# The delta rule's gate columns with TensorE's operands exchanged

## The reference, cut to what matters

```
h = rms_norm(x, mix_pre_norm[l])
proj = h @ w_in                      # (256, 1024) @ (1024, D_IN)
(dn_qkv, dn_z, dn_b, dn_a, ...) = jnp.split(proj, ...)   # dn_b, dn_a: 4 columns each
qkv = silu(causal_depthwise_conv(dn_qkv, dn_conv))
beta = sigmoid(dn_b)
g = -exp(dn_A_log) * softplus(dn_a + dn_dt_bias)
o_dn = gated_delta_rule(q, k, v, beta, g)
```

## Time and profile before

| what | us |
|---|---|
| three runs, median | 1917.99 |
| three runs, lowest and highest | 1915.57, 1919.57 |
| the profiled execution | 1917.77 |
| its span in the profile | 1916.0 |

### The profile page before, as it was taken

How to read it: one execution, slowest core, us unless ns; L and a number is a source line. 1 busy time by engine, 2 the same in 40 slices (tenths; PEclk the granted TensorE clock), 3 DMA queues, 4 the chain that set the end, 5 groups by cost and what they waited for, 6 DMA issues and landing times.

```text
span 1916.0 us, 35058 instructions
## 1 busy us (share of the span) xinstructions
PE 1888.3 (99%) x14788; PEld 1806.2 (94%) x14788; DVE 1252.2 (65%) x1678; ACT 956.3 (50%) x1381; POOL 308.2 (16%) x176
## 2 busy tenths in 40 slices
PE   7999999999999999999999999999999999999998
PEld 7999998998899999999989999999999899999998
DVE  6884567665689545777648775576647694567643
ACT  5634456444563345564445445555534445556533
POOL 0050221000003103200001352320001352221000
PEclk9999999999999999999999999999999999999999
DMA  6443344666545323555565553456655663445553
GB/s 227 160 143 111 112 154 153 205 195 209 163 135 165 111 99 122 201 173 190 193 195 176 183 187 122 133 181 190 191 187 171 218 193 115 136 169 187 186 188 100
DMA packets 92156, 317.50 MB, mean 166 GB/s; under 512 B 11744, under 2 KB 12896, under 8 KB 91744
## 3 DMA queue, kind: packets, MB, share of 16 engines
q1 hardware_dynamic: 91424, 314.69, 50.2%
q10 hardware_dynamic: 576, 0.57, 0.1%
HBM read 304.99 MB, written 1.05 MB: 160 GB/s over the span
## 4 chain that ended last, share of the span: by engine, by line
PE 84%; DVE 11%; ACT 2%; DMA 1%; issue 1%; SPq 0%; DVEq 0%; ACTq 0%
PE bank L2001 82%; DVE wlo L1126 4%; DVE area L1126 3%; DVE area L1132 1%; DMA raw<-in_weights 1%; ACT area L630 1%; PE bank L2512 1%; DVE hl L1132 1%; DVE xT L1132 1%; ACT whi L636 1%; PE bank L2220 1%; DVE area L1645 1%; DVE area L1643 0%; PE bank L2530 0%; ACT L618 0%
## 5 line engine op out<-in xcount | busy, mean ns | idle before, releaser
L1126 DVE TENSOR_TENSOR wlo<-raw,whi 128x1024 fp32r<-128x1024 f32 x518 | 666.3, 1301 | 402.6 <-ACT whi L636 402.2
L2001 PE MATMUL bank<-hh,whi 128*128 128x256 f32 x2928 | 834.5, 286 | 15.1 <-DVE wlo L1126 11.7
L2001 PE MATMUL bank<-hh,wlo 128*128 128x256 f32 x2928 | 818.2, 280 | 0.0
L2001 PE MATMUL bank<-hl,whi 128*128 128x256 f32 x2928 | 811.3, 280 | 0.0
L636 ACT CAST whi<-raw 128x1024 fp32r<-128x1024 f32 x572 | 589.4, 1046 | 415.7 <-PE bank L2001 369.9
L2001 PEld LDWEIGHTS bank<-hh,whi 128*128 128x128 f32 x2928 | 555.7, 190 | 28.4 <-DVE wlo L1126 15.1
L2001 PEld LDWEIGHTS bank<-hl,whi 128*128 128x128 f32 x2928 | 555.2, 191 | 1.9 <-issue 1.9
L2001 PEld LDWEIGHTS bank<-hh,wlo 128*128 128x128 f32 x2928 | 556.0, 190 | 0.0
L1781 POOL TENSOR_TENSOR area<-area 128x512 f32<-128x512 f32 (+4 forms) x86 | 136.7, 1596 | 567.8 <-DVE area L1132 249.8
L1781 POOL TENSOR_TENSOR wlo<-raw,whi 128x1024 fp32r<-128x1024 f32 x54 | 134.3, 2488 | 427.9 <-ACT whi L636 427.9
L2001 PE MATMUL bank<-area 128*128 128x128 f32 (+5 forms) x1544 | 199.9, 288 | 1.2 <-DVE area L1196 0.7
(11 more groups left out here) (127 smaller groups left out, 1918.3 us busy)
## 6 DMA issues: line engine op xcount, KB each, us to landing
raw<-in_weights SPq DMA_DIRECT2D x572, 512.0 KB, 4.1
area<-area SPq DMA_DIRECT2D x96, 64.0 KB, 3.6
area<-area SPq DMA_DIRECT2D x16, 128.0 KB, 4.0
cst<-in_const SPq DMA_DIRECT2D x1, 1188.0 KB, 8.3
cst<-in_const SPq DMA_DIRECT2D x1, 1024.5 KB, 6.9
xT<-in_x SPq DMA_DIRECT2D x4, 256.0 KB, 8.1
out<-xT SPq DMA_DIRECT2D x4, 256.0 KB, 2.9
area<-in_lev SPq DMA_DIRECT2D x2, 384.0 KB, 6.6
```

Source lines behind the costliest of these rows:

```text
L1126: return v.tensor_tensor(dst, x, y, op)
L2001: return e.matmul(ps, x, y, start=start, stop=stop, skip_group_check=skip)
```

## The change

The gate weights become the stationary operand, 16 columns (high and low side by side) for `hh` and 8 for `hl`, and 256 tokens are the other operand: 16 matmuls, whose sum is a 16 x 256 array in bank 1, rows 0 to 7 high by all, rows 8 to 15 low by high. They run after step 2 (behind the norm's sum) instead of after step 3. VectorE copies the 16 x 256 array to `ABR` (in plain fp32) in its hook, for which it waits. After step 3 TensorE multiplies each half of `ABR` as weights (16 x 128) with a 16 x 8 matrix, two identity matrices over each other, which transposes and adds the two halves in one; it is appended to `small` in 8 columns, so that tile grows from 576 to 584 columns. VectorE's product with the factor reads bank 1 at once. The cast and the subtraction of `SW` move out of the hooks, to between steps 1 and 2.

```diff
-N_SMALL = 64 + 512
+N_SMALL = 64 + 512 + 8
...
+        ABR = SM[0:16, 0:256]
...
                 def hook():
                     factor(norm)
-                    a.wait_ge(s_small[L], 16)
-                    a.copy(SW[:, :, 0:8], sm3).then_inc(*a_dn.up("SW", L))
...
                 next(qkv)
                 next(qkv)
+                a.wait_ge(s_small[L], 16)
+                a.copy(SW[:, :, 0:8], sm3).then_inc(*a_dn.up("SW", L))
                 next(qkv)
                 next(qkv)
...
                 def hook():
                     factor(norm)
-                    v.wait_ge(*a_dn.at("SW", L))
-                    tt(SW[:, :, 8:16], sm3, SW[:, :, 0:8].bitcast(F32), OP.subtract).then_inc(*v_dn.up("SW", L))
+                    v.wait_ge(*e_dn.at("abrow", L))
+                    v.tensor_copy(ABR, bank[1][0:16, 0:256]).then_inc(*v_dn.up("abrow", L))
...
                 next(qkv)
                 next(qkv)
+                v.wait_ge(*a_dn.at("SW", L))
+                tt(SW[:, :, 8:16], sm3, SW[:, :, 0:8].bitcast(F32), OP.subtract).then_inc(*v_dn.up("SW", L))
                 next(qkv)
                 next(qkv)
-                two = bank[1][:, 0:32].rearrange("p (s c) -> p s c", s=2)
                 v.wait_ge(*e_dn.at("ab", L))
-                v.tensor_copy(tmp2, two[:, :, 8:16]).then_inc(*v_dn.up())
-                v.wait_ge(*v_dn.now())
-                tt(AB2, two[:, :, 0:8], tmp2, OP.add).then_inc(*v_dn.up("absum", L))
-                v.wait_ge(*v_dn.now())
                 v.wait_ge(*v_norm.at("turned", norm))
-                tt(AB2, AB2, wide(RST[:, :], 2, 8), OP.mult).then_inc(*v_dn.up("ab", L))
+                tt(AB2, bank[1][:, 256:272].rearrange("p (s c) -> p s c", s=2), wide(RST[:, :], 2, 8), OP.mult).then_inc(*v_dn.up("ab", L))
...
                 next(qkv)
                 next(qkv)
                 next(qkv)
+                e.wait_ge(*v_dn.at("SW", L))
+                fresh(1, v_dn.at("ab", L))
+                for k in range(8):
+                    mm(bank[1][0:16, 0:T], SW[:, k, :], hh[:, k, :], k == 0, False, True)
+                    x = mm(bank[1][0:8, 0:T], SW[:, k, 0:8], hl[:, k, :], False, k == 7, True)
+                x.then_inc(*e_dn.up("abrow", L))
                 next(qkv)
-                e.wait_ge(*v_dn.at("SW", L))
-                fresh(1, v_dn.at("absum", L))
+                e.wait_ge(*v_dn.at("abrow", L))
                 for s in range(2):
-                    for k in range(8):
-                        mm(bank[1][:, 16 * s:16 * s + 16], hh[:, k, 128 * s:128 * s + 128], SW[:, k, :], k == 0, False, True)
-                        x = mm(bank[1][:, 16 * s:16 * s + 8], hl[:, k, 128 * s:128 * s + 128], SW[:, k, 0:8], False, k == 7, True)
+                    x = mm(bank[1][:, T + 8 * s:T + 8 * s + 8], ABR[:, 128 * s:128 * s + 128], small[0:16, 576:584], True, True)
                 x.then_inc(*e_dn.up("ab", L))
...
+        small[l][0:16, 576:584] = np.tile(np.eye(8, dtype=np.float32), (2, 1))
```

More of the change, by code:

```diff
@@ L398, in program @@
         u1, u2 = SM[:, 128:136], SM[:, 144:152]
-        AB2, tmp2 = (SM[:, c:c + 16].rearrange("p (s c) -> p s c", s=2) for c in (192, 224))
+        AB2 = SM[:, 192:208].rearrange("p (s c) -> p s c", s=2)
         AB = SM[:, 192:208].rearrange("p (s c) -> p c s", s=2)
+        ABR = SM[0:16, 0:256]
         sm3 = small[:, 0:64].rearrange("p (k c) -> p k c", c=8)
```

## The result

The changed kernel takes 1937.96 us (median of 4 runs, 1934.9 to 1938.49), the kernel before beside it 1916.78 (4 runs, 1913.67 to 1919.57): ratio 1.0117, 95% interval 1.0098 to 1.0137. The profiled execution took 1937.57, its span is 1935.8. I had said 1914.8, in a range from 1909.5 to 1918.8.

What follows compares the result with a forecast made beforehand. TensorE, busy 99%, was taken as the bound, with VectorE limiting its gain at the end of `qkv`. 1917.77 minus 1.1 (layer 0) and 2.0 (layer 1) gave 1914.7, plus 0.2 for the median: 1914.8 us, range 1909.5 to 1918.8.

Steps and rivals of the forecast that it cites:

- The 8 more columns of `small` are 4 KB: nothing.: Transfer of the enlarged `small`: the 8 added columns, 4 KB, were said to cost nothing.
- The row matmuls: TensorE, gates in `qkv`: the 16 new matmuls with 256 columns streamed take 1.9 us in all.
- The two transposing ones: TensorE, gates: two matmuls with fp32 weights and 8 columns streamed take 0.4 us together.
- Rival (3): Gates: row matmuls run at the fp32 rate, 7.2 us for 1.9; slower, 1925.3 us; chance 8%.
- The copy: VectorE's hook: copying the 16 x 256 array takes 0.43 us alone, 0.35 before a next one; 0.6 allowed.
- The product at 32.6 and the evacuation of pair 4 at 36.3 without idle: VectorE, layer 0: product near 32.6 us, evacuation near 36.3 with its earlier 1.04 us idle gone.
- The clock: TensorE at the gates: clock staying at 1.00 also saves 2.7 us in layer 0, 2.2 in layer 1.
- Rival (1): Clock falls anyway, before chunk 9 or in the narrow matmuls; 1918.5 us, no change; chance 17%.
- the price of a fall: TensorE: one fall of the clock was said to cost 3.4 us.
- VectorE's cap: `qkv`: VectorE limits the gain to 1.1 us in layer 0, 2.0 in layer 1; TensorE waits 3.5 in layer 0.
- Rival (2): `qkv`: VectorE does not hold TensorE back; 4.6 + 5.0 = 9.6 us gained, 1908.2 us; chance 15%.
- a smaller gain of 1.0: If the old clock is low for less long, the 1.04 and 1.07 us idle can't be had; 1.0 left.

Runs made afterwards that it cites:

- run 9: Changed kernel with every tile at its place of before, `RST` moved into unused columns of `par`: 1914.47 us against 1916.24 for the kernel before, ratio 0.9989.
- run 1: Kernel before with `small` made 584 columns wide and nothing else: 1939.76 us against 1912.27, ratio 1.0143.
- run 2: Changed kernel with 8 more unused columns, `small` at 592: 1945.14 us, ratio 1.0177.
- run 6: Changed kernel with `small` at 608 columns, `hh` at distance 64 from `whi`: 1930.58 us, ratio 1.0079.
- run 12: run 9 plus GpSimd instead of VectorE making `wlo` of chunks 9 and 11 in both layers: 1917.07 us against 1917.87, ratio 0.9995.
- run 3: Kernel before with `small` at 592 columns, `hh` at distance 0 from `whi`: 1949.26 us, ratio 1.0196.
- run 7: Kernel before with 64 bytes left free ahead of `whi`, so all tiles behind move along, distance still 192: 1917.6 us against 1914.44, ratio 1.0006.
- run 11: Kernel before with 160 bytes left free ahead of `hh`, distance 96 from `whi`: 1956.36 us, ratio 1.0208.
- run 5: Kernel before with `small` at 608 columns, `hh` at distance 64 from `whi`: 1930.1 us, ratio 1.007.

## Why the prediction was wrong

The step that failed is one sentence: "The 8 more columns of `small` are 4 KB: nothing." I had priced the transfer only. The columns also push every tile behind `small` by 32 bytes, which made the pitch of some 10,700 matmuls 0.9 to 2.5 ns longer and that of 720 wide ones 2.7; by the medians that cost 23.5 us (changed kernel against run 9) to 27.5 (run 1). None of my cases or rivals had an effect outside the two `qkv` stages, and the range held only those. Shown by run 1 (the size without the change: the whole loss) and run 9 (the change without the shift: no loss).

The other steps, by run 9 where all lies as before:

- The row matmuls: 1.9 us said, 1.9 found. The two transposing ones: 0.4 said, 0.53 found. Rival (3), the fp32 rate: refuted, 0.12 us per matmul.
- The copy: 0.35 to 0.43 said, 0.41 found, with 0.34 to the next start. On its 16 partitions it took as long as the reduce of 128 x 256 right before it (0.42).
- The product at 32.6 and the evacuation of pair 4 at 36.3 without idle: found at 32.66 and 36.24.
- The clock: stays up at the gates in both layers, as in the changed kernel and runs 2 and 6. Rival (1) gave the wait before chunk 9 as the danger. That wait was 1.44 us (I had said about 2), the clock stayed at 1.00; run 12 made it 2.67 (2.6 in layer 1), and the clock fell to 0.50 both times. None of the rows I had read shows a fall of the clock behind a wait, the longest at full clock being 1.03 us; that a wait is a danger was my guess. The 3.4 us that I gave as the price of a fall are those of the earlier trace rows, (0.46 + 0.22) x 5; that fall begins at 30.4, so 1.46 us of it lie within the gate matmuls.
- VectorE's cap: TensorE's 4.6 us of layer 0 became 1.1, and new waits for `wlo` appeared (2.5 us in 3 waits in layer 0, 2.9 in 4 in layer 1; I had said 3.5 for layer 0). Rival (2), with 1908.2, is refuted. Run 12 did not lift the cap, so that VectorE's chain and nothing behind it sets it is argued from the waits, not shown.
- What the exchange is worth depends on what it is compared with. It also takes away a fall of the clock that is not of one length and does not come each time: 6.8 us in both layers of the profiled execution of before, about 3.4 in both of run 1, 6.8 and 3.4 in run 3, 6.8 and none in runs 7 and 11. I had allowed for that, as a smaller gain of 1.0. Layer 1 shows it: from cast 150 to cast 162 the kernel before takes 46.25 us, run 9 takes 43.86, and run 7, which has the old gates but no fall there, 43.98. At equal places the medians differ by -1.8 (224; run 1 was not timed beside it, and by cast 568 of the two traces it is -3.4), -4.1 (0), +0.5 (64, within the spread) and -1.8 us (192).

## What to carry to other kernels

When an edit changes the size of an SBUF tile, ask what lies behind it: every operand there moves, and in a kernel bound by TensorE, as this one, a few ns of pitch in ten thousand matmuls can outweigh what the edit was for: here 2.5 ns in 8784 of them, 22 us, against a gain of 1.8. Put new tiles last or into free space, and before judging an edit run the old kernel with the new sizes and nothing else. Run both often enough: the kernel before alone took between 1901 and 1925 us in these measurements, so that a gain of 2 us shows only in a median of many. Compare pitches by the distance of starts over a whole trace, stage by stage; busy times per instruction overlap and hide the difference (here 288 ns against 286, with a pitch of 118.3 against 115.8).

## What was not expected of the hardware

- The pitch of 256-column fp32r matmuls at full clock depends on the distance, modulo 256 bytes, at which streamed operand and weights start: 115.8 to 120.0 ns in the table. At 0 and 96 it is nearly even, 119.4 to 120.3 in stretches of 20 us (runs 3 and 11); it changes at 192 between 113.3 and 117.8 (the kernel before, runs 7 and 9), at 64 between 113.3 and 118.1 (runs 5 and 6). One 512-column form ranks the distances otherwise (226.8 at 0, 234.2 at 96).
- Run 7 against run 3 shows that the distance counts, and not the place of `hh` alone: ratios to the kernel before of 1.0006 and 1.0196, 32 us in 1950, with `hh` at the same address in both.
- Open: what makes the pitch change levels at distances 192 and 64, within one execution and from one to the next; why the distances rank as they do; distance 32, which no run had; and what in TensorE depends on the distance.
- A stream of 256 columns against 16 or 8 columns of weights costs the same 0.12 us as against 128, and in all five traces that have it (the changed kernel, runs 2, 6, 9 and 12) the clock stayed at 1.00 during and right behind it, in both layers. During or behind the 32 matmuls with 8 or 16 columns streamed against 128 it fell to 0.50 in 16 of 18 cases (two layers in nine traces of the old gates), but not always. In layer 0 of the kernel before it fell 2.7 us into them: their pitch is 0.11 us up to 30.38 and 0.21 from there. The two without a fall are layer 1 of runs 7 and 11; in run 7 the old gates start at 530.56 and the windows read:

```profile
530.56 0.17 PE L2002 MATMUL bank<-SW,hh 128*128 128x16 f32 x1
```

```profile
530.00:535.00 5.00, 5.00 (x47) 1.00 0.31 120
535.00:540.00 5.00, 5.00 (x45) 1.00 0.44 144
```

No version ran clearly below run 9, which is 0.11% (0.02 to 0.20) below the kernel before.
